# High halves from the scaled tile with the bias at once, low halves two tiles behind the scaling, and the first slot behind each norm waiting tile by tile

## The chip, the core and the metric

The kernel runs on one core of a Trainium2 chip. Its engines work side by side, each through its own list of instructions: TensorE (PE; its weight loads are shown as PEld), VectorE (DVE), ScalarE (ACT), GpSimd (POOL) and SyncE (SP), which only issues DMAs here. They wait for each other by semaphores. The metric is the device time of one execution in microseconds (us), as the median of several runs.

## The reference

One inference step of a two-layer decoder: 256 new tokens of a prompt and 8 tokens of running samples go through the same weights. Layer 0 is a gated DeltaNet and a dense SwiGLU, layer 1 a short gated convolution and an expert SwiGLU (two of eight). Behind each of the four sublayers stands a norm over the 1024 features:

```
def layer_norm(x, g, b):
    mu = mean(x); var = mean((x - mu) ** 2)
    return (x - mu) * rsqrt(var + LN_EPS) * g + b

hp = layer_norm(ALPHA * hp + mixer(hp), ln_g[i, 0], ln_b[i, 0])     # 256 prompt tokens
hp = layer_norm(ALPHA * hp + channel_mixer(hp), ln_g[i, 1], ln_b[i, 1])
# hs, the 8 sample tokens, in the same way
```

Two of these four are touched: the first norm of layer 0, behind which the gate and up projections of the dense SwiGLU follow (x @ w_gu), and the second, behind which the input projection of the short convolution follows (x @ w_in).

## The kernel before, in words

The 264 tokens (256 + 8) stand side by side as columns, the 1024 features as 8 tiles of 128 partitions. `xres[:, k, :]` is feature tile k of the residual stream, 128x264 in float32. To keep float32 accuracy on TensorE each operand is a sum of a high half (rounded by the engine that writes it, type fp32r) and a low half, the rest. A product is three matmuls: weights high by x high, weights high by x low, weights low by x high.

Weights come in slots of 1 MB (128x2048). SP loads slot n into one of 7 buffers `raw`, ScalarE makes `high` in one of 3 buffers (`split_high`, L335), VectorE makes `low` (`split_low`, L340), and TensorE consumes a slot in `dense_slot`. A dense slot has 2 groups (t) of 128 output features. A group first runs over the 8 feature tiles with a pair of matmuls each, L354 (with `xh`, the high half of x) and L355 (with `xl`, the low half), and then over the 8 tiles again with L359 (low weights). When a slot is done, `slot_used` counts up; that frees buffers, so ScalarE and VectorE split the slot 3 further on and SP loads the one 7 further on. `dense_slot` takes an `arrive` function that can wait before each pair of the first group; before the change only the out projection of layer 0 used it.

The norm in this transposed layout: TensorE sums the 8 tiles with a matrix of ones (L1704, mean), VectorE subtracts the mean (L1186), ScalarE squares (L793), TensorE sums again (L1708, variance), ScalarE forms rstd by a logarithm and an exponential (L795, L797), for which it loads a table. Then comes the tail of the norm, which the change is about:

- VectorE scales the 8 tiles by gamma and rstd (L1189), counting `scaled`;
- ScalarE adds the bias in place (L800), counting `x_new`, and one tile behind copies to the high half `xh` (L805, the last at L808), counting `xh_ready`;
- VectorE, once all 8 tiles are scaled, subtracts to get the low half `xl` (L1194), counting `xl_ready`;
- TensorE waits for all high and all low halves (L1712 and L1713 in layer 0, L1747 and L1748 in layer 1) and only then goes on.

Behind the first norm TensorE then transposes the last rows of the DeltaNet's input (L1721, eight small matmuls), which ScalarE copies out (L818, `tail_sb`); the second slot waits for these copies. Then come 11 pairs of gate and up slots. GpSimd waits for all of `x_new` of the first norm (L517) before it loads the state of the samples, which ScalarE reads at L834. The order on every engine is written out by hand: it is the order of the code.

Of the kernel before, what the change touches and what calls it, by code (L numbers as in the profile page):

```python
# [8 lines left out]
KT = D // 128  # L9
# [51 lines left out]
def hybrid_step(nc, x_prompt, x_sample, state_gdn_S, state_gdn_conv, state_sconv, ln_g, ln_b, gdn_w_in,  # L61
# [8 lines left out]
    with ExitStack() as ctx:  # L70
# [546 lines left out]
        def _(act):  # L617
# [168 lines left out]
                act.wait_ge(slot_used, n + 1)  # L786
                split_high(act, n + SPLIT)

            def layer_norm(l, split):
                act.preload_act_table_set("natural_log")  # L790
                for k in range(KT):
                    act.wait_ge(xc_ready, 8 * l + k + 1)
                    act.activation(lnsq[:, k, :], xres[:, k, :], ACT.Square).then_inc(lnsq_ready, 1)  # L793
                act.wait_ge(var_psum, l + 1)
                act.activation(rvar[:, :], bank[5][:, 0:N], ACT.Ln, scale=1.0 / D, bias=eps[:, 1:2]).then_inc(var_inv, 1)  # L795
                act.wait_ge(var_inv, l + 1)
                act.activation(rstd[:, :], rvar[:, :], ACT.Exp, scale=-0.5).then_inc(var_root, 1)  # L797
                for k in range(KT):
                    act.wait_ge(scaled, 8 * l + k + 1)
                    act.activation(xres[:, k, :], xres[:, k, :], ACT.Identity, bias=vecs[:, k, 4 + l:5 + l])\  # L800
                        .then_inc(x_new, 1)
                    if split:
                        if k:
                            act.wait_ge(x_new, 8 * l + k)
                            act.activation(xh[:, k - 1, :], xres[:, k - 1, :], ACT.Copy).then_inc(xh_ready, 1)  # L805
                if split:
                    act.wait_ge(x_new, 8 * l + 8)
                    act.activation(xh[:, KT - 1, :], xres[:, KT - 1, :], ACT.Copy).then_inc(xh_ready, 1)  # L808

            layer_norm(0, True)  # L810

            act.wait_ge(hist_out, 48)
            for i in range(FF // 256):
# [22 lines left out]
            for n in range(DOWN0, SCI0):  # L836
                act.wait_ge(slot_used, n + 1)
                split_high(act, n + SPLIT)
            layer_norm(1, True)

            for i in range(D // 256):
                n = SCI0 + 2 * i
# [75 lines left out]
        def _(dve):  # L918
# [253 lines left out]
                    add_residual(2 * (n - OUT0) + t, 2 * (n % 2) + t)  # L1172
                split_low(dve, n + SPLIT)

            def layer_norm(l, split):
                dve.wait_ge(mean_psum, l + 1)
                if l == 0:
                    dve.wait_ge(zero_out, 16 * (JOBS + 2))
                    dve.wait_ge(gate_out, 48)
                    dve.wait_ge(hist_out, 48)  # L1180
                if l == 1:
                    dve.wait_ge(tail_out, 32)
                step(dve.tensor_scalar(mu[:, :], bank[4][:, 0:N], 1.0 / D, None, ALU.mult))
                step.wait()
                for k in range(KT):
                    dve.tensor_tensor(xres[:, k, :], xres[:, k, :], mu[:, :], ALU.subtract).then_inc(xc_ready, 1)  # L1186
                dve.wait_ge(var_root, l + 1)
                for k in range(KT):
                    dve.scalar_tensor_tensor(xres[:, k, :], xres[:, k, :], vecs[:, k, l:l + 1], rstd[:, :],  # L1189
                                             ALU.mult, ALU.mult).then_inc(scaled, 1)  # L1190
                if split:
                    for k in range(KT):
                        dve.wait_ge(xh_ready, 8 * (l + 2) + k + 1)
                        dve.tensor_tensor(xl[:, k, :], xres[:, k, :], xh[:, k, :].bitcast(F32), ALU.subtract)\  # L1194
                            .then_inc(xl_ready, 1)

            layer_norm(0, True)
            for i in range(FF // 256):
                n = GU0 + 2 * i
                dve.wait_ge(slot_used, n + 1)  # L1200
# [20 lines left out]
            for n in range(DOWN0, SCI0):  # L1221
# [2 lines left out]
                    for d in range(KT):  # L1224
                        add_residual(d, d)
                split_low(dve, n + SPLIT)
            layer_norm(1, True)

            dve.wait_ge(const_ready, 6)
            for i in range(D // 256):  # L1230
# [238 lines left out]
        def _(pe):  # L1469
# [230 lines left out]
            def layer_norm(l):  # L1700
# [7 lines left out]
                    last = pe.matmul(bank[5][:, 0:N], ones[:, :], lnsq[:, k, :], start=k == 0, stop=k == KT - 1)  # L1708
                last.then_inc(var_psum, 1)

            layer_norm(0)
            pe.wait_ge(xh_ready, 24)  # L1712
            pe.wait_ge(xl_ready, 24)  # L1713
            for i in range(FF // 256):
                if i >= 2:
                    pe.wait_ge(gate_silu, 2 * (i - 1))
                    pe.wait_ge(h_ready, 2 * (i - 1))
                if i < 3:
                    for b in range(2):
                        for t in range(4):  # L1720
                            last = pe.transpose(bank[4 * (i % 2) + 2 + b][0:11, 128 * t:128 * t + 128],  # L1721
                                                utail[:, 8 * i + 4 * b + t, :], idn)
                        last.then_inc(tail_psum, 1)
                dense_slot(pe, GU0 + 2 * i, 4 * (i % 2), xh, xl)
                if i < 3:
                    pe.wait_ge(tail_sb, 2 * i + 2)
                dense_slot(pe, GU0 + 2 * i + 1, 4 * (i % 2) + 2, xh, xl)
# [16 lines left out]
                last.then_inc(slot_used, 1)  # L1744
            pe.wait_ge(res_ready, 16)
            layer_norm(1)
            pe.wait_ge(xh_ready, 32)  # L1747
            pe.wait_ge(xl_ready, 32)  # L1748
            for i in range(D // 256):
                if i >= 2:  # L1750
                    pe.wait_ge(c_copied, 2 * (i - 1))
                    pe.wait_ge(u_ready, 2 * (i - 1))
                dense_slot(pe, SCI0 + 2 * i, 4 * (i % 2), xh, xl)
                dense_slot(pe, SCI0 + 2 * i + 1, 4 * (i % 2) + 2, xh, xl)
            for i in range(D // 256):
                pe.wait_ge(c_copied, 6 if i < 2 else 8)
# [168 lines left out]
```

## Time and profile before

| | |
|---|---|
| median of 3 runs | 1688.25 us (1687.16 to 1688.6) |
| the profiled execution | 1687.96 us |
| its span, from the first to the last instruction | 1686.2 us |
| TensorE busy in the span | 1589.6 us, 94% |
| VectorE, ScalarE, GpSimd busy | 1272.0, 1049.7, 96.5 us |
| mean granted clock of TensorE | 0.966 |

All rows below come from the one profiled execution, with times from the start of its span. Busy times overlap, and a busy TensorE isn't one at its peak: what a stage is bound by is read from who waits last in it. The granted clock has two levels, 1.00 (2.4 GHz) and 0.50 (1.2 GHz); a value between them is a stretch in which it changed.

### The profile page before, as it was taken

How to read it: one execution, taken by the hardware profiler on the slowest of the kernel's cores; microseconds unless marked ns; L12 is line 12 of the kernel's file. 1: busy time of each engine (PE TensorE's matmuls, PEld its weight loads, DVE VectorE, ACT ScalarE, POOL GpSimd, SP SyncE). 2: the span in 40 equal slices, each digit the busy share in tenths (PEclk: the TensorE clock that was granted, in tenths of full speed). 3: DMA queues.
4: the chain of work that ended last, by engine and by line, in shares of the span. 5: the costliest groups of instructions: out<-in, count | busy, mean ns of one | idle time of the engine just before them, and what ended most of it. 6: DMA issues, size and time to landing. Idle time of an engine off the chain costs nothing.

```text
span 1686.2 us, 23688 instructions
## 1 busy us (share of the span) xinstructions
PE 1589.6 (94%) x8997; PEld 1379.7 (82%) x8997; DVE 1272.0 (75%) x1234; ACT 1049.7 (62%) x959; POOL 96.5 (6%) x151
## 2 busy tenths in 40 slices
PE   7999997799996999999999999999999999999991
PEld 6889997799996998887887887887887887887881
DVE  5685545377534656888888888888889889889887
ACT  4981424466434333777777777777777777777772
POOL 3105000011000001000000000000000000002001
PEclk9998999899998997999999999999999999999996
DMA  9647603389553552999999999999999999999991
GB/s 269 213 133 229 251 2 113 125 265 320 193 179 123 184 165 82 388 374 340 391 367 347 388 367 350 385 367 350 385 366 351 382 368 353 380 364 359 395 367 64
DMA packets 228273, 480.19 MB, mean 285 GB/s; under 512 B 9660, under 2 KB 69068, under 8 KB 227913
## 3 DMA queue, kind: packets, MB, share of 16 engines
q1 hardware_dynamic: 215904, 438.92, 72.8%
q0 software_dynamic: 11216, 40.06, 7.0%
q10 hardware_dynamic: 1096, 0.41, 0.2%
q8 instruction: 41, 0.67, 0.2%
q14 instruction: 16, 0.13, 0.0%
HBM read 452.82 MB, written 26.77 MB: 284 GB/s over the span
## 4 chain that ended last, share of the span: by engine, by line
PE 88%; ACT 5%; DVE 4%; DMA 1%; issue 1%; DVEq 0%; SPq 0%; ACTq 0%; POOLq 0%
PE bank L1847 12%; PE bank L1848 12%; PE bank L1851 12%; PE bank L1876 11%; PE bank L354 6%; PE bank L355 6%; PE bank L359 6%; PE bank L1882 6%; ACT high L335 2%; PE bank L1606 1%; PE bank L1737 1%; PE bank L1738 1%; PE bank L1743 1%; PE bank L1627 1%; PE bank L1859 1%; DVE low L340 1%
## 5 line engine op out<-in xcount | busy, mean ns | idle before, releaser
L340 DVE TENSOR_TENSOR low<-raw,high 128x2048 fp32r<-128x2048 f32 x408 | 931.2, 2290 | 249.9 <-ACT high L335 249.7
L335 ACT ACTIVATE high<-raw 128x2048 fp32r<-128x2048 f32 x408 | 779.7, 1916 | 284.4 <-PE bank L1851 104.7
L1847 PE MATMUL bank<-high,xgh 128*128 128x512 f32 x896 | 359.7, 401 | 0.0
L1848 PE MATMUL bank<-high,xgl 128*128 128x512 f32 x896 | 355.5, 397 | 0.0
L1851 PE MATMUL bank<-low,xgh 128*128 128x512 f32 x896 | 246.0, 396 | 0.0
L354 PE MATMUL bank<-xh,high 128*128 128x264 f32 x864 | 228.7, 297 | 16.8 <-ACT xh L808 9.3
L355 PE MATMUL bank<-xl,high 128*128 128x264 f32 x864 | 225.6, 294 | 0.0
L1851 PEld LDWEIGHTS bank<-low,xgh 128*128 128x128 f32 x896 | 168.9, 189 | 41.4
L1847 PEld LDWEIGHTS bank<-high,xgh 128*128 128x128 f32 x896 | 169.5, 189 | 38.7
L1848 PEld LDWEIGHTS bank<-high,xgl 128*128 128x128 f32 x896 | 168.8, 188 | 38.8
L354 PEld LDWEIGHTS bank<-xh,high 128*128 128x128 f32 x864 | 171.1, 198 | 19.1 <-ACT xh L808 9.6
L355 PEld LDWEIGHTS bank<-xl,high 128*128 128x128 f32 x864 | 171.3, 198 | 1.0 <-issue 1.0
L1876 PE MATMUL bank<-high,hth 128*128 128x512 f32 x448 | 141.4, 397 | 8.1 <-DVE htl L1414 8.1
L1876 PE MATMUL bank<-high,htl 128*128 128x512 f32 x448 | 140.5, 395 | 0.0
L359 PE MATMUL bank<-xh,low 128*128 128x264 f32 x864 | 124.5, 287 | 1.3 <-DVE low L340 1.3
L1882 PE MATMUL bank<-low,hth 128*128 128x512 f32 x448 | 122.3, 394 | 0.0
L359 PEld LDWEIGHTS bank<-xh,low 128*128 128x128 f32 x864 | 114.6, 192 | 1.6 <-DVE low L340 1.6
L1876 PEld LDWEIGHTS bank<-high,hth 128*128 128x128 f32 x448 | 83.5, 188 | 28.8 <-issue 10.0
L1882 PEld LDWEIGHTS bank<-low,hth 128*128 128x128 f32 x448 | 84.4, 188 | 20.2
L1876 PEld LDWEIGHTS bank<-high,htl 128*128 128x128 f32 x448 | 84.5, 189 | 19.8
L899 ACT ACTIVATE sgx<-bank 128x512 f32<-128x512 f32 x56 | 33.5, 599 | 42.6 <-PE bank L1851 42.5
L597 POOL TENSOR_TENSOR flag<-flag 128x1 f32<-128x1 f32 x1 | 2.2, 2218 | 880.5 <-DMA tok<-ysb 880.5
(370 smaller groups left out, 1473.5 us busy)
## 6 DMA issues: line engine op xcount, KB each, us to landing
raw<-in_moe_w_gu_dram SPq DMA_DIRECT2D x224, 1024.0 KB, 5.3
raw<-in_moe_w_down_dram SPq DMA_DIRECT2D x115, 1024.0 KB, 5.4
raw<-in_ffn_w_gu_dram SPq DMA_DIRECT2D x22, 1024.0 KB, 7.0
raw<-in_gdn_w_in_dram SPq DMA_DIRECT2D x16, 1024.0 KB, 8.5
tok<-zeros POOLq DMA_DIRECT2D x26, 512.0 KB, 17.4
raw<-in_sc_w_in_dram SPq DMA_DIRECT2D x12, 1024.0 KB, 5.1
raw<-in_ffn_w_down_dram SPq DMA_DIRECT2D x11, 1024.0 KB, 5.0
tok<-ysb SPq DMA_DIRECT2D x9, 512.0 KB, 6.0
```

The source lines that it names most:

```text
L335: eng.activation(high[:, n % SPLIT, :], raw[:, n % RAW, :], ACT.Copy).then_inc(high_ready, 1)
L340: eng.tensor_tensor(low[:, n % RAW, :], raw[:, n % RAW, :], high[:, n % SPLIT, :].bitcast(F32), ALU.subtract).then_inc(low_ready, 1)
L354: pe.matmul(out, wh[:, k, f], act_h[:, k, :], start=k == 0, stop=False)
L355: pe.matmul(out, wh[:, k, f], act_l[:, k, :], start=False, stop=False)
L359: last = pe.matmul(out, wl[:, k, f], act_h[:, k, :], start=False, stop=k == KT - 1)
L899: act.activation(sgx[:, u % 2, :], bank[2 * (u % 2)][:, :], ACT.Silu).then_inc(sgx_ready, 1)
L1606: last = pe.matmul(heads(4 * c + g)[:, h % 4, :], AT[:, c, h, :], T[:, c, h, :], start=True, stop=True)
L1847: pe.matmul(out, xgh[:, 4 * kh + k, :], wh[:, k, :], start=kh + k == 0, stop=False)
L1848: pe.matmul(out, xgl[:, 4 * kh + k, :], wh[:, k, :], start=False, stop=False)
L1851: last = pe.matmul(out, xgh[:, 4 * kh + k, :], wl[:, k, :], start=False, stop=kh == 1 and k == 3)
L1876: pe.matmul(bank[4 + g][:, :], src[:, u % 2, hs], wh[:, k, 512 * g:512 * g + 512], start=u + kh + k == 0 and src is hth, stop=False)
L1882: last = pe.matmul(bank[4 + g][:, :], hth[:, u % 2, hs], wl[:, k, 512 * g:512 * g + 512], start=False, stop=u == UNITS - 1 and kh + k == 2)
```

## The change

In the tail of the norm ScalarE makes the high half of tile k straight from the scaled tile, with the bias added in the same pass. VectorE makes the low half of tile k - 2 right behind the scaling of tile k, as (scaled tile + bias) - high half. ScalarE adds the bias to `xres` in place only after all eight high halves, tile k once low half k has been made. TensorE doesn't wait for the whole norm any more: the first group of the first slot waits before each pair for that tile's halves, and the transposes behind the first norm wait for nothing of it.

```diff
@@ ScalarE, layer_norm(l)
                 for k in range(KT):
                     act.wait_ge(scaled, 8 * l + k + 1)
+                    act.activation(xh[:, k, :], xres[:, k, :], ACT.Identity, bias=vecs[:, k, 4 + l:5 + l]).then_inc(xh_ready, 1)
+                for k in range(KT):
+                    act.wait_ge(xl_ready, 8 * (l + 2) + k + 1)
                     act.activation(xres[:, k, :], xres[:, k, :], ACT.Identity, bias=vecs[:, k, 4 + l:5 + l])\
                         .then_inc(x_new, 1)
-                    if split:
-                        if k:
-                            act.wait_ge(x_new, 8 * l + k)
-                            act.activation(xh[:, k - 1, :], xres[:, k - 1, :], ACT.Copy).then_inc(xh_ready, 1)
-                if split:
-                    act.wait_ge(x_new, 8 * l + 8)
-                    act.activation(xh[:, KT - 1, :], xres[:, KT - 1, :], ACT.Copy).then_inc(xh_ready, 1)
@@ VectorE, layer_norm(l)
                 dve.wait_ge(var_root, l + 1)
+                def low_half(k):
+                    dve.wait_ge(xh_ready, 8 * (l + 2) + k + 1)
+                    dve.scalar_tensor_tensor(xl[:, k, :], xres[:, k, :], vecs[:, k, 4 + l:5 + l], xh[:, k, :].bitcast(F32),
+                                             ALU.add, ALU.subtract).then_inc(xl_ready, 1)
+
                 for k in range(KT):
                     dve.scalar_tensor_tensor(xres[:, k, :], xres[:, k, :], vecs[:, k, l:l + 1], rstd[:, :],
                                              ALU.mult, ALU.mult).then_inc(scaled, 1)
-                if split:
-                    for k in range(KT):
-                        dve.wait_ge(xh_ready, 8 * (l + 2) + k + 1)
-                        dve.tensor_tensor(xl[:, k, :], xres[:, k, :], xh[:, k, :].bitcast(F32), ALU.subtract)\
-                            .then_inc(xl_ready, 1)
+                    if k >= 2:
+                        low_half(k - 2)
+                low_half(KT - 2)
+                low_half(KT - 1)
@@ TensorE
+            def norm_arrives(l):
+                def arrive(k):
+                    pe.wait_ge(xh_ready, 8 * (l + 2) + k + 1)
+                    pe.wait_ge(xl_ready, 8 * (l + 2) + k + 1)
+                return arrive
+
             layer_norm(0)
-            pe.wait_ge(xh_ready, 24)
-            pe.wait_ge(xl_ready, 24)
...
-                dense_slot(pe, GU0 + 2 * i, 4 * (i % 2), xh, xl)
+                dense_slot(pe, GU0 + 2 * i, 4 * (i % 2), xh, xl, norm_arrives(0) if i == 0 else None)
...
             layer_norm(1)
-            pe.wait_ge(xh_ready, 32)
-            pe.wait_ge(xl_ready, 32)
...
-                dense_slot(pe, SCI0 + 2 * i, 4 * (i % 2), xh, xl)
+                dense_slot(pe, SCI0 + 2 * i, 4 * (i % 2), xh, xl, norm_arrives(1) if i == 0 else None)
```

On VectorE the tail of the first norm stands like this before (var_root says that rstd is there):

```order
L1189 SCALAR_TENSOR_TENSOR xres<-xres,vecs,rstd 128x264 [waits var_root]
L1189 SCALAR_TENSOR_TENSOR xres<-xres,vecs,rstd 128x264 x7
L1194 TENSOR_TENSOR xl<-xres,xh 128x264 [waits xh_ready] x8
```

and like this after, where the scaling is L1190 and the low half L1186:

```order
L1190 SCALAR_TENSOR_TENSOR xres<-xres,vecs,rstd 128x264 [waits var_root]
L1190 SCALAR_TENSOR_TENSOR xres<-xres,vecs,rstd 128x264 x2
L1186 SCALAR_TENSOR_TENSOR xl<-xres,vecs,xh 128x264 [waits xh_ready]
L1190 SCALAR_TENSOR_TENSOR xres<-xres,vecs,rstd 128x264
L1186 SCALAR_TENSOR_TENSOR xl<-xres,vecs,xh 128x264 [waits xh_ready]
...
L1190 SCALAR_TENSOR_TENSOR xres<-xres,vecs,rstd 128x264
L1186 SCALAR_TENSOR_TENSOR xl<-xres,vecs,xh 128x264 [waits xh_ready] x3
```

Each low half from the first on now stands between two scalings, and a wait for ScalarE stands ahead of each scaling from the fourth on. On TensorE, from the variance sums of the first norm on, before:

```order
L1708 MATMUL bank<-lnsq,ones 128x264 [waits lnsq_ready] x8
L1721 MATMUL bank<-ident,utail 11x128 [waits xl_ready,xh_ready]
L1721 MATMUL bank<-ident,utail 11x128 x7
L354 MATMUL bank<-xh,high 128x264 [waits high_ready]
L355 MATMUL bank<-xl,high 128x264
L354 MATMUL bank<-xh,high 128x264
L355 MATMUL bank<-xl,high 128x264
```

and after (the transposes are L1725):

```order
L1708 MATMUL bank<-lnsq,ones 128x264 [waits lnsq_ready] x8
L1725 MATMUL bank<-ident,utail 11x128 x8
L354 MATMUL bank<-xh,high 128x264 [waits xl_ready,xh_ready,high_ready]
L355 MATMUL bank<-xl,high 128x264
L354 MATMUL bank<-xh,high 128x264 [waits xl_ready,xh_ready]
L355 MATMUL bank<-xl,high 128x264
```

The wait for the halves has moved from the transposes to the pairs, and every pair of the first group has its own. On ScalarE, after, from rstd on:

```order
L797 ACTIVATE rstd<-rvar 128x264 [waits var_inv]
L800 ACTIVATE xh<-xres,vecs 128x264 [waits scaled] x8
L803 ACTIVATE xres<-xres,vecs 128x264 [waits xl_ready] x8
L814 ACTIVATE tail_nat<-bank 11x512 [waits tail_psum,hist_out]
L814 ACTIVATE tail_nat<-bank 11x512 [waits tail_psum]
L820 ACT_TABLE_LOAD
L820 ACTIVATE sg<-bank 128x264 [waits slot_used]
```

Before, the two passes of a tile alternated; now the eight passes in place stand behind the eight high halves, with the tail copies behind them as before.

## Rows read from the trace of the kernel before

**Rows 1.** The page's span, and groups by line: busy, mean ns, idle before.

```profile
span 1686.2 us, 23688 instructions
L359 PE MATMUL bank<-xh,low 128*128 128x264 f32 x864 | 124.5, 287 | 1.3 <-DVE low L340 1.3
L1189 DVE SCALAR_TENSOR_TENSOR xres<-xres,vecs,rstd 128x264 f32<-128x264 f32 x16 | 6.6, 487 | 10.1 <-ACT rstd L797 10.1
```

**Rows 2.** Waits, 285 to 320 us: total, times, longest.

```profile
PE bank L1721 <- DVE xl L1194: 9.3, 1, 9.3
```

**Rows 3.** Timeline of VectorE, first norm: start, duration, instruction, count, idle before.

```profile
302.01 3.32 DVE L1189 SCALAR_TENSOR_TENSOR xres<-xres,vecs,rstd 128x264 f32<-128x264 f32 x8 [5.91 <-ACT rstd L797]
305.25 1.86 DVE L1194 TENSOR_TENSOR xl<-xres,xh 128x264 fp32r<-128x264 f32 x5
...
308.11 0.78 DVE L1194 TENSOR_TENSOR xl<-xres,xh 128x264 fp32r<-128x264 f32 x2 [0.28 <-ACT xh L805]
```

**Rows 4.** Timeline of ScalarE, first norm and the start of the gate slots.

```profile
302.54 0.92 ACT L800 ACTIVATE xres<-xres,vecs 128x264 f32<-128x264 f32 x2 [0.56 <-DVE xres L1189]
...
303.68 0.50 ACT L800 ACTIVATE xres<-xres,vecs 128x264 f32<-128x264 f32 x1
304.08 0.41 ACT L805 ACTIVATE xh<-xres 128x264 fp32r<-128x264 f32 x1
...
307.98 0.41 ACT L808 ACTIVATE xh<-xres 128x264 fp32r<-128x264 f32 x1
...
311.54 1.28 ACT L824 ACT_TABLE_LOAD   x1
...
327.40 1.05 ACT L818 ACTIVATE tail_nat<-bank 11x512 f32<-11x512 f32 x2
...
339.99 2.44 ACT L834 ACTIVATE dB<-dB,kS 128x128 f32<-128x128 f32 x8
```

**Rows 5.** Timeline of TensorE, first norm.

```profile
294.20 5.52 PE L1708 MATMUL bank<-lnsq,ones 128*128 128x264 f32 x16 [2.11 <-ACT lnsq L793]
309.03 1.87 PE L1721 MATMUL bank<-ident,utail 128*11 128x128 f32 x8 [9.31 <-DVE xl L1194]
310.55 0.57 PE L354 MATMUL bank<-xh,high 128*128 128x264 f32 x1
...
314.21 1.42 PE L359 MATMUL bank<-xh,low 128*128 128x264 f32 x8
315.47 0.28 PE L354 MATMUL bank<-xh,high 128*128 128x264 f32 x1
315.59 0.28 PE L355 MATMUL bank<-xl,high 128*128 128x264 f32 x1
```

**Rows 6.** Timeline of VectorE, second norm.

```profile
525.67 3.32 DVE L1189 SCALAR_TENSOR_TENSOR xres<-xres,vecs,rstd 128x264 f32<-128x264 f32 x8 [4.22 <-ACT rstd L797]
...
531.77 0.78 DVE L1194 TENSOR_TENSOR xl<-xres,xh 128x264 fp32r<-128x264 f32 x2 [0.28 <-ACT xh L805]
```

**Rows 7.** Timeline of TensorE, second norm.

```profile
532.64 0.56 PE L354 MATMUL bank<-xh,high 128*128 128x264 f32 x1 [9.26 <-ACT xh L808]
533.00 0.42 PE L355 MATMUL bank<-xl,high 128*128 128x264 f32 x1
533.22 0.42 PE L354 MATMUL bank<-xh,high 128*128 128x264 f32 x1
...
536.30 1.34 PE L359 MATMUL bank<-xh,low 128*128 128x264 f32 x8
```

**Rows 8.** Windows of 1 us, first norm: busy (x count) by engine, clock, DMA, GB/s.

```profile
297.00:298.00 1.00, 1.00 (x5) 0.76 (x3) 0.00 (x0) 0.00 (x0) 0.00 (x0) 0.62 0.00 0
...
304.00:305.00 1.00, 0.00 (x0) 0.00 (x0) 1.00 (x4) 1.00 (x4) 0.00 (x0) 0.80 0.00 0
...
314.00:315.00 1.00, 1.00 (x7) 1.00 (x7) 0.00 (x0) 0.00 (x0) 0.00 (x0) 0.58 1.06 315
```

**Rows 9.** The same, second norm (PE, PEld, DVE, ACT, POOL in that order).

```profile
536.00:537.00 1.00, 1.00 (x8) 1.00 (x7) 0.00 (x0) 0.00 (x0) 0.00 (x0) 0.65 0.82 307
```

**Rows 10.** Timeline of GpSimd, first norm.

```profile
308.46 0.89 POOL L520 DMA_DIRECT2D s0f<-in_state_gdn_S_dram  x1 [50.02 <-ACT xres L800]
```

More of the change, by code:

```diff
@@ L787, in _, with layer_norm @@
                 split_high(act, n + SPLIT)
-            def layer_norm(l, split):
+            def layer_norm(l):
                 act.preload_act_table_set("natural_log")
@@ L799, in layer_norm @@
                     act.wait_ge(scaled, 8 * l + k + 1)
+                    act.activation(xh[:, k, :], xres[:, k, :], ACT.Identity, bias=vecs[:, k, 4 + l:5 + l]).then_inc(xh_ready, 1)
+                for k in range(KT):
+                    act.wait_ge(xl_ready, 8 * (l + 2) + k + 1)
                     act.activation(xres[:, k, :], xres[:, k, :], ACT.Identity, bias=vecs[:, k, 4 + l:5 + l])\
                         .then_inc(x_new, 1)
-                    if split:
-                        if k:
-                            act.wait_ge(x_new, 8 * l + k)
-                            act.activation(xh[:, k - 1, :], xres[:, k - 1, :], ACT.Copy).then_inc(xh_ready, 1)
-                if split:
-                    act.wait_ge(x_new, 8 * l + 8)
-                    act.activation(xh[:, KT - 1, :], xres[:, KT - 1, :], ACT.Copy).then_inc(xh_ready, 1)
-            layer_norm(0, True)
+            layer_norm(0)
             act.wait_ge(hist_out, 48)
@@ L838, in _ @@
                 split_high(act, n + SPLIT)
-            layer_norm(1, True)
+            layer_norm(1)
             for i in range(D // 256):
@@ L1173, in _, with layer_norm @@
                 split_low(dve, n + SPLIT)
-            def layer_norm(l, split):
+            def layer_norm(l):
                 dve.wait_ge(mean_psum, l + 1)
@@ L1190, in layer_norm @@
                                              ALU.mult, ALU.mult).then_inc(scaled, 1)
-                if split:
-                    for k in range(KT):
-                        dve.wait_ge(xh_ready, 8 * (l + 2) + k + 1)
-                        dve.tensor_tensor(xl[:, k, :], xres[:, k, :], xh[:, k, :].bitcast(F32), ALU.subtract)\
-                            .then_inc(xl_ready, 1)
-            layer_norm(0, True)
+                    if k >= 2:
+                        low_half(k - 2)
+                low_half(KT - 2)
+                low_half(KT - 1)
+            layer_norm(0)
             for i in range(FF // 256):
@@ L1226, in _ @@
                 split_low(dve, n + SPLIT)
-            layer_norm(1, True)
+            layer_norm(1)
             dve.wait_ge(const_ready, 6)
```

## The prediction, as it was made before the changed kernel ran

> **What bounds the kernel now.** I read the waits of the stretch around the first norm first, then the timelines of VectorE, ScalarE and TensorE in it, then the same for the second norm, and last the stretches of 1 us for the granted clock. In a dense slot TensorE hardly waits: its 864 matmuls with low halves (L359) were held 1.3 us in all by a split [rows 1]. Behind the first norm it stands still for 9.3 us, and what ends this is the last low half of x [rows 2]. So the tail of each norm lies on the path that sets the end, and a microsecond gained there on TensorE should stay gained, since the slots behind it are bound by TensorE.
>
> The tail runs like this in the first norm. VectorE scales eight tiles from 302.01 and only then makes low halves from 305.25; the last two end at 308.11 + 0.78 = 308.89 [rows 3]. It is not VectorE alone: ScalarE does two passes a tile, bias in place and then the high half [rows 4], and its last high half is what the last low halves wait for. TensorE starts at 309.03 with eight transposes of the tail rows, reaches the slot's first pair at 310.55 after 1.52 us, and its first low-weight matmul (L359) at 314.21 [rows 5]. The second norm has no transposes: scaling from 525.67, last low half at 531.77 + 0.78 = 532.55 [rows 6], first pair at 532.64, L359 at 536.30 [rows 7].
>
> **The change, part by part.** I work out when L359 of the first group starts, since from there on the instructions are the same as before.
>
> VectorE: eight scalings of mean 487 ns [rows 1] take 3.32 us in a row, so one starts (3.32 - 0.487) / 7 = 0.405 us behind the other [rows 3]. The new low half has the same kind of operands (two tensors and a column of scalars) and isn't in the trace. Bounds: the old low half starts (1.86 - 0.43) / 4 = 0.358 us apart [rows 3], and without any overlap it would be 0.487. I take 0.405, that of the scaling, the same form of instruction. The row is now S0 S1 S2 L0 S3 L1 ... S7 L5 L6 L7, 16 instructions. L7 starts 15 x 0.405 = 6.08 behind the first and ends 0.49 later: 302.01 + 6.56 = 308.57 in the first norm, 525.67 + 6.56 = 532.23 in the second. That is only 0.32 us earlier than before in each: VectorE becomes the limit of the tail, and the larger gain must come from TensorE. With 0.487 for all, L7 ends at 302.01 + 16 x 0.487 = 309.80, 1.23 us later in each norm, 2.5 in all. With 0.358 for the low halves, ScalarE's relay (next) leaves at most 0.15 us in each, 0.3 in all.
>
> ScalarE: high half k is now one pass with the bias, 0.50 us long, a next one 0.40 behind it [rows 4]; the scaled tiles come 0.81 apart, so it keeps up. Does the relay stall VectorE? S0 ends at 302.50, high half 0 runs 302.54 to 303.04, and L0 is due at 302.01 + 3 x 0.405 = 303.23. S7 starts at 302.01 + 12 x 0.405 = 306.87 and ends at 307.36, its high half ends at about 307.90, L7 is due at 308.09. There is 0.15 to 0.19 us to spare, so two tiles of distance are just enough, and I put the stall at nothing. A full relay at each tile would take 0.49 + 0.04 + 0.50 + 0.04 + 0.49 = 1.56 us, one of the rivals.
>
> TensorE: pair k starts when its low half is there. At the low clock a pair takes 2 x 0.22 = 0.44 us [rows 7], against 0.81 between arrivals, so only the last pairs queue: L5, L6, L7 come 0.405 apart. From the end of the last low half to L359 I take what the lone first pair of the second norm shows: 532.64 - 532.55 = 0.09, then 0.36 to its second matmul, then 0.22 to the next, 0.67 us [rows 6, 7]. L359 starts at 308.57 + 0.67 = 309.24 instead of 314.21, 4.97 earlier, and at 532.23 + 0.67 = 532.90 instead of 536.30, 3.40 earlier. Sum 8.37 us. Of the 4.97, 1.52 are the transposes: they no longer stand behind the wait for xl and run in the idle time after the variance sums.
>
> The clock takes part of that back. It falls at about 304.6 [rows 8] in the idle time, when the new pairs have barely begun; so pairs and L359 start at the low level (1.2 GHz). Before, it rose again at 314.84 (0.58 in that microsecond means 0.84 us low) and at 536.70 [rows 8, 9]: L359 had just begun, only 0.63 and 0.40 us behind its start were low. A matmul takes 0.220 us low and 0.122 high [rows 5], so a low microsecond loses 0.445: 0.28 and 0.18 us. The rises that I can read came 3.6 us (294.20 to 297.76), 4.1 us (532.64 to 536.70) and 5.8 us (309.03 to 314.84) behind the first matmul after an idle time [rows 5, 7, 8, 9]. Now TensorE works without a pause from pair 5 on, 307.85 and 531.51 (L5's end and 0.09). I take the middle one, 4.1: rises at 311.9 and 535.6, 2.7 us behind L359, a loss of 1.2 us in each norm against 0.28 and 0.18 before: 1.0 and 1.0 given back. Bounds: with 3.6, 0.8 in each; with 5.8, 1.7 and 1.8; and if the spaced pairs already bring the rise, nothing is lost and the 0.46 of before is won besides.
>
> [...]
>
> What is moved behind. ScalarE writes x in place after all high halves, pass k waiting for L k: from 307.81, 0.405 apart, the last from about 310.64 to 311.15; before, it had finished at 308.39. Behind it are queued the two tail copies, 1.05 together [rows 4], to 312.2, and a table load of 1.28 to 313.5. TensorE's second slot waits for these copies; its first slot ends at 309.24 + 8 x 0.22, then some four matmuls low and twenty high, about 314.3, or 313.15 with the clock high throughout. So 1 to 2 us cover the later copies, and I cost them at nothing; the SiLU behind the table load is not asked for by TensorE until two pairs of slots later. GpSimd's state loads wait for the last x: they leave 2.7 us later than at 308.46 [rows 10], and ScalarE first reads them at 339.99 [rows 4], some 25 us behind. SP's queue waits on slots alone and moves with TensorE.
>
> Sum: 8.37 - 2.0 = 6.4 us. The profiled execution took 1687.96 us (span 1686.2, and 1.76 around it), which gives 1681.6; it lies 0.29 below the median of the runs, so by the median it would be 1681.9.
>
> **The rivals.** Late clock: the rise is as late as the slowest row in both norms, 5.8 us. Then 4.4 us behind L359 are low, 1.97 lost in each, 3.5 more than before, 4.9 us gained: 1683.1. For it: the first norm did this, with the transposes ahead. Against: two of three rises came sooner.
> Early clock: the spaced pairs, some 0.44 us of work in 0.81, bring the rise before L359: 8.8 gained, 1679.1. Nothing in the trace shows a stretch like that at the low level, for or against.
> Serial relay: VectorE stands still for ScalarE at every tile, 1.56 instead of 0.81 us a step. Five such steps lie ahead of L5, 5 x 0.75 = 3.75 in each norm, 7.5 in all against the 6.4: 1.1 slower, 1689.1, no change that can be measured. For it: the margin is only 0.15 us. Against: a wait that is already satisfied shows no cost, the old low halves with one each started 0.358 apart [rows 3].
> Slower: the same relay with slower handovers. Above 0.81 + 6.4 / 10 = 1.45 us a step the kernel loses, above 0.81 + (6.4 + 3.4) / 10 = 1.79 by more than 0.2%. At 1.9 us it is 10 x 1.09 = 10.9 against 6.4, 4.5 slower: 1692.5. Three instructions of 0.49, 0.50 and 0.49 leave 0.42 for two handovers, 0.21 each, where the rows show 0.04 (302.50 to 302.54).
>
> **How the numbers follow.** Forecast 0.60, late clock 0.17, early clock 0.12, serial relay 0.08, slower 0.03. The time is 1681.6. The range goes from the early clock, 1679.0, to 1684.5, which takes in the late clock with 1.4 us of the bound on VectorE's pace; beyond it lie the relays and the worst of that pace. The measurement tells about 0.2%, 3.4 us, from no change. Faster than that: forecast, early and nearly all of the late clock, 0.88; within it: serial relay and the rest, 0.09; slower 0.03.
>
> **What would show it.** In the profile after: low halves and scalings alternate on VectorE 0.40 apart, with no idle over 0.1 us, the last ending 6.5 to 6.6 us behind the first scaling; pairs on TensorE 0.8 apart; the transposes right behind the variance sums; L359 at 7.2 us behind the first scaling; the granted clock back at 2.4 GHz about 2.7 us behind L359's start; no wait for the tail copies. I am wrong if VectorE shows gaps in front of low halves, if the clock rises outside 0 to 4.4 us behind L359, or if TensorE in the first slots stands for ScalarE.

## The result, and the profile after

| | median | runs | profiled execution | its span | mean granted clock |
|---|---|---|---|---|---|
| before | 1690.01 us | 6 (1687.16 to 1691.93) | 1687.96 | 1686.2 | 0.966 |
| changed | 1678.46 us | 6 (1674.81 to 1680.17) | 1677.33 | 1675.6 | 0.970 |

The ratio is 0.9931, with a 95% interval of 0.9915 to 0.9946: 11.7 us less by the ratio, 11.55 by the medians, where 6.4 were forecast. The time of 1678.46 lies below the range, which began at 1679.0. The median of before is over six runs now, three of them beside the changed kernel.

The tail of the norm does what was worked out. VectorE in the first norm, timeline of the changed kernel (start, duration, instruction, count, idle before), against [rows 3]:

```profile
304.63 1.30 DVE L1190 SCALAR_TENSOR_TENSOR xres<-xres,vecs,rstd 128x264 f32<-128x264 f32 x3 [5.91 <-ACT rstd L797]
305.85 0.48 DVE L1186 SCALAR_TENSOR_TENSOR xl<-xres,vecs,xh 128x264 fp32r<-128x264 f32 x1
306.26 0.49 DVE L1190 SCALAR_TENSOR_TENSOR xres<-xres,vecs,rstd 128x264 f32<-128x264 f32 x1
...
309.49 0.48 DVE L1190 SCALAR_TENSOR_TENSOR xres<-xres,vecs,rstd 128x264 f32<-128x264 f32 x1
309.90 1.30 DVE L1186 SCALAR_TENSOR_TENSOR xl<-xres,vecs,xh 128x264 fp32r<-128x264 f32 x3
```

Scalings and low halves start 0.40 us apart and no row has an idle time; the last ends at 309.90 + 1.30 = 311.20, 6.57 us behind the first scaling (6.56 forecast). ScalarE, against [rows 4]:

```profile
305.16 1.33 ACT L800 ACTIVATE xh<-xres,vecs 128x264 fp32r<-128x264 f32 x3 [0.56 <-DVE xres L1190]
306.78 0.52 ACT L800 ACTIVATE xh<-xres,vecs 128x264 fp32r<-128x264 f32 x1 [0.29 <-DVE xres L1190]
...
310.43 3.34 ACT L803 ACTIVATE xres<-xres,vecs 128x264 f32<-128x264 f32 x8
313.68 1.05 ACT L814 ACTIVATE tail_nat<-bank 11x512 f32<-11x512 f32 x2
```

From the fourth on it waits 0.29 us for each scaled tile, so it has room. TensorE, against [rows 5]:

```profile
302.18 1.04 PE L1725 MATMUL bank<-ident,utail 128*11 128x128 f32 x8
306.48 0.36 PE L354 MATMUL bank<-xh,high 128*128 128x264 f32 x1 [3.26 <-ACT xh L800]
306.68 0.28 PE L355 MATMUL bank<-xl,high 128*128 128x264 f32 x1
307.29 0.56 PE L354 MATMUL bank<-xh,high 128*128 128x264 f32 x1 [0.33 <-ACT xh L800]
...
311.98 1.96 PE L359 MATMUL bank<-xh,low 128*128 128x264 f32 x8
313.74 0.42 PE L354 MATMUL bank<-xh,high 128*128 128x264 f32 x1
...
315.85 1.13 PE L359 MATMUL bank<-xh,low 128*128 128x264 f32 x8
```

The last row is L359 of the second group, which in the kernel before stands here:

```profile
317.42 1.15 PE L359 MATMUL bank<-xh,low 128*128 128x264 f32 x8
```

The transposes stand behind the variance sums, pairs come 0.81 apart, and L359 starts 311.98 - 304.63 = 7.35 us behind the first scaling, where it was 314.21 - 302.01 = 12.20 [rows 3, 5] and 7.23 was forecast (from the end of the last low half to L359 it is 0.78 us, not 0.67). In the second norm (timelines of VectorE and TensorE) it is 7.35 again, against 10.63 [rows 6, 7]:

```profile
525.32 1.30 DVE L1190 SCALAR_TENSOR_TENSOR xres<-xres,vecs,rstd 128x264 f32<-128x264 f32 x3 [4.22 <-ACT rstd L797]
...
532.67 1.96 PE L359 MATMUL bank<-xh,low 128*128 128x264 f32 x8
```

So L359 came 4.85 and 3.28 us earlier (4.97 and 3.40 forecast). The granted clock, in windows of 1 us (busy by engine, clock, DMA share, GB/s), against [rows 8, 9]:

```profile
314.00:315.00 1.00, 1.00 (x10) 1.00 (x10) 0.00 (x0) 0.98 (x3) 0.53 (x1) 0.97 0.00 0
...
535.00:536.00 1.00, 1.00 (x7) 1.00 (x6) 0.00 (x0) 0.00 (x0) 0.24 (x1) 0.54 0.97 225
```

It is back at 2.4 GHz at 314.06 and 535.92, 2.1 and 3.3 us behind L359 (2.7 forecast in both). In these terms nothing is off by more than 0.6 us. The rest of the 11.7 us is somewhere else, and comparing stage by stage shows where: most of it at the gather of the expert rows, 340 us behind the first norm, which the change doesn't touch. There TensorE picks the token rows for the experts by 48 small matmuls with a one-hot matrix; behind them come 20 transposes and then the first expert matmul. TensorE's timeline there, before and then changed:

```profile
650.56 13.32 PE L1825 MATMUL bank<-onehot,xn 128*128 128x128 f32 x48 [0.81 <-DVE onehot L1350]
...
667.99 0.78 PE L1847 MATMUL bank<-high,xgh 128*128 128x512 f32 x1
```

```profile
646.66 8.48 PE L1827 MATMUL bank<-onehot,xn 128*128 128x128 f32 x48 [0.80 <-DVE onehot L1350]
...
658.18 0.49 PE L1849 MATMUL bank<-high,xgh 128*128 128x512 f32 x1 [0.71 <-DVE xgl L1398]
```

The same 48 matmuls take 13.3 or 8.5 us. Windows of before and of the changed kernel say why (the granted clock is the third number from the end):

```profile
645.00:646.00 1.00, 1.00 (x7) 1.00 (x6) 1.00 (x1) 0.00 (x0) 0.00 (x0) 0.54 0.00 0
...
652.00:653.00 1.00, 1.00 (x7) 0.76 (x6) 0.90 (x7) 0.00 (x0) 1.00 (x1) 0.88 0.00 0
...
669.00:670.00 1.00, 1.00 (x4) 0.81 (x3) 1.00 (x1) 0.00 (x0) 0.00 (x0) 0.59 0.00 0
```

```profile
641.00:642.00 1.00, 1.00 (x8) 1.00 (x7) 0.97 (x3) 0.10 (x1) 0.00 (x0) 0.63 0.00 0
...
648.00:649.00 1.00, 1.00 (x8) 0.76 (x7) 0.86 (x7) 0.00 (x0) 0.91 (x1) 1.00 0.00 0
```

Before, the clock rose at 645.92, fell again at 652.76, 2.2 us into the gather, and stayed at 1.2 GHz for 17 us, though TensorE was never idle in them. In the changed kernel it rose at 641.74 and stayed up. From the gather's start to the first expert matmul it is 17.43 us before and 11.52 after, and 0.71 of the 11.52 is now a wait for VectorE's low half of the gathered rows: with the clock high TensorE is no longer the one that comes last there. Another low stretch, at the first slot of the convolution's output projection (from 608.38 before), has gone too, and one at the start of the down projection (from 443.76 after) is new:

```profile
608.00:609.00 1.00, 1.00 (x8) 1.00 (x8) 0.88 (x1) 1.00 (x3) 0.00 (x0) 0.69 1.04 406
```

```profile
443.00:444.00 1.00, 0.45 (x3) 0.45 (x3) 0.50 (x2) 1.00 (x2) 0.00 (x0) 0.88 0.40 115
...
606.00:607.00 1.00, 1.00 (x9) 1.00 (x10) 1.00 (x1) 0.64 (x2) 0.07 (x1) 1.00 1.04 406
```

### The profile page after: what moved, and what is told of

Same layout as the page of the kernel before. It is cut to its first block, busy times and chain, and to the rows that moved or that the text cites. A ratio compares the mean times of both kernels' runs of the same rounds, so it can differ in the third digit from the quotient of the medians.

```text
span 1675.6 us, 23702 instructions
## 1 busy us (share of the span) xinstructions
PE 1589.7 (95%) x8997; PEld 1378.2 (82%) x8997; DVE 1272.3 (76%) x1234; ACT 1052.4 (63%) x959; POOL 96.3 (6%) x151
## 4 chain that ended last, share of the span: by engine, by line
PE 88%; DVE 5%; ACT 4%; DMA 1%; issue 1%; DVEq 0%; SPq 0%; ACTq 0%; POOLq 0%
PE bank L1849 13%; PE bank L1853 13%; PE bank L1850 13%; PE bank L1878 11%; PE bank L354 6%; PE bank L359 6%; PE bank L355 6%; PE bank L1884 6%; ACT high L335 2%; PE bank L1741 1%; DVE low L340 1%; PE bank L1742 1%; PE bank L1606 1%; PE bank L1747 1%; PE bank L1627 1%; PE bank L1861 1%
## 5 line engine op out<-in xcount | busy, mean ns | idle before, releaser
L359 PE MATMUL bank<-xh,low 128*128 128x264 f32 x864 | 126.2, 290 | 1.4 <-DVE low L340 1.4
L359 PEld LDWEIGHTS bank<-xh,low 128*128 128x128 f32 x864 | 116.2, 194 | 1.6 <-DVE low L340 1.6
L1878 PEld LDWEIGHTS bank<-high,hth 128*128 128x128 f32 x448 | 83.5, 188 | 28.8 <-issue 10.0
```

Source lines behind the costliest of these rows:

```text
L359: last = pe.matmul(out, wl[:, k, f], act_h[:, k, :], start=False, stop=k == KT - 1)
L1878: pe.matmul(bank[4 + g][:, :], src[:, u % 2, hs], wh[:, k, 512 * g:512 * g + 512], start=u + kh + k == 0 and src is hth, stop=False)
```

## The experiments

Theory 1: the norms save what the rows gave, some 6 us, and the rest is the clock at the gather. 1a, added later: whether it falls there depends on the moment at which TensorE gets there behind the last rise of the clock. Its rivals: theory 2, the norms alone save the whole 11 us, by the new order of the halves; 1b, only the idle gap ahead of the gather counts. The `keep_running(n, b)` of the edits issues n filler transposes of an identity matrix into bank b, whose result no one reads; the kernel before has some already.

**TensorE's part alone** (shown for the first norm; the second has the same edit).

```diff
 # kernel before
-            pe.wait_ge(xh_ready, 24)
-            pe.wait_ge(xl_ready, 24)
-                dense_slot(pe, GU0 + 2 * i, 4 * (i % 2), xh, xl)
+                dense_slot(pe, GU0 + 2 * i, 4 * (i % 2), xh, xl, norm_arrives(0) if i == 0 else None)
```

> TensorE's part alone: the kernel before, but the first slot behind each norm waits tile by tile and the transposes wait for nothing of the norm; ScalarE and VectorE as before. The low halves then come as before, the last at 6.88 us behind the first scaling, with the last three 0.36 and 0.7 apart. L359 at 6.88 + 0.67 = 7.6 us behind the first scaling, against 12.2 (first norm) and 10.6 (second) before and 7.35 in the changed kernel. Theory 1 (the saving at the norms is what was predicted, some 6 us, and the rest comes from the clock at the gather of the expert rows, which falls or not with the moment that stage is reached): 5 to 6 us less than before from the norms, and another 6 where the gather's clock holds; its profile tells which, gather (L1825) 13.3 us low or 8.5 us high. Theory 2 (the norms alone save the whole 11 us, by the new order of the halves): clearly less gain here than in the changed kernel, even where the gather takes the same time.

Measured: 1678.77 us, ratio 0.9936 (0.9919 to 0.9952), the gain of the whole change within the intervals. L359 7.70 and 7.48 us behind the first scaling, 4.50 and 3.15 earlier than before where the whole change has 4.85 and 3.28; gather 8.48 us. So TensorE's part, the wait tile by tile with the transposes ahead of it, is nearly all of it.

**The halves alone** (again in both norms).

```diff
 # changed kernel
             layer_norm(0)
+            pe.wait_ge(xh_ready, 24)
+            pe.wait_ge(xl_ready, 24)
-                dense_slot(pe, GU0 + 2 * i, 4 * (i % 2), xh, xl, norm_arrives(0) if i == 0 else None)
+                dense_slot(pe, GU0 + 2 * i, 4 * (i % 2), xh, xl)
```

> The halves alone: ScalarE and VectorE as in the changed kernel, TensorE waits for the whole norm as before. The last low half ends 6.6 instead of 6.9 us behind the first scaling, so L359 0.2 to 0.3 us earlier in each norm. Theory 1: 0.4 to 0.6 us of gain at the norms, which no run can tell, and all further difference is the gather's, 0 or 5 to 7 us, with the matmuls of the gather in the profile at 8.5 or 13.3 us. Theory 2: several us of gain with the gather as before.

Measured: 1689.05 us, ratio 0.9994 (0.9984 to 1.0004). Its gather, in TensorE's timeline, is the slow one:

```profile
647.59 13.39 PE L1825 MATMUL bank<-onehot,xn 128*128 128x128 f32 x48 [0.81 <-DVE onehot L1350]
```

The order of the halves by itself gives 0.1 us by the medians; the interval allows up to 2.7. In its first norm the first pair comes 8.22 us behind the first scaling instead of 8.54, the 0.3 expected. L359 comes 1.2 earlier there, and the rest of that is the clock, which rose at 311.80, 1.1 us ahead of L359. That the halves save the 11 us falls with these two; that the norms do, with the next two.

**Feeding TensorE ahead of the gather**, in the kernel before and in the changed one.

```diff
             pe.wait_ge(xn_ready, 6)
-            keep_running(12, 6)
+            keep_running(20, 6)
```

> The kernel before with 20 instead of 12 filler transposes ahead of the gather, which fill the 0.8 us in which TensorE waits for onehot there. Theory 1: the clock doesn't fall at the gather, which takes 8.5 instead of 13.3 us, and the first expert slot starts some 6 us earlier: 5 to 7 us less than before, 0.1 to 0.3 of it lost to the filler. Theory 2: the clock at the gather costs nothing that counts, or falls all the same: within 1 us of before.

> The changed kernel with the same 20 fillers. Theory 1: its gather was mostly at the high clock already, so within 1.5 us of the changed kernel's 1678.5, and 6 us (5 to 7.5) below the kernel before with the fillers: that is the change's own saving. Theory 2: 10 to 12 us below the kernel before with the fillers.

Measured: before, fed, 1684.70 us, ratio 0.9971 (0.9961 to 0.9981); changed, fed, 1678.23, ratio 0.9934 (0.9922 to 0.9947). The gather of before, fed:

```profile
654.05 8.48 PE L1825 MATMUL bank<-onehot,xn 128*128 128x128 f32 x48
```

Filling 0.8 us of idle time gives the kernel before 4.5 us, a little less than the 5 to 7 expected, and the changed one nothing that can be told. The difference of the two fed kernels, 6.5 us, is what the change is worth with the gather at one clock, to some 2.5 us either way by the two intervals; the forecast was 6.4. The low stretches elsewhere are not the same in the two, see below.

**Only the transposes moved ahead of the wait.**

```diff
 # kernel before
             layer_norm(0)
-            pe.wait_ge(xh_ready, 24)
-            pe.wait_ge(xl_ready, 24)
...
+                if i == 0:
+                    pe.wait_ge(xh_ready, 24)
+                    pe.wait_ge(xl_ready, 24)
                 dense_slot(pe, GU0 + 2 * i, 4 * (i % 2), xh, xl)
```

> The kernel before with one edit: behind the first norm the eight transposes stand ahead of the wait for the halves. Theory 1 (the norms save what the sum of rows says): 1.5 us leave the path there, L359 at 10.7 instead of 12.2 us behind the first scaling, less what more low clock behind it costs, so 0.5 to 1.5 us of gain, with the gather as before at 13.3 us. Theory 2 (an arrival at the gather that is earlier by any amount frees its clock): 6 us or more.

Measured: 1682.87 us, ratio 0.9959 (0.9944 to 0.9975), about 7 us for an edit that takes 1.9 us off L359 (10.31 us behind the first scaling). I expected 1.5 at most: the miss has the same cause as that of the prediction, the gather took 8.48 us. By its time alone this run meets the rival in that expectation, that any earlier arrival at the gather frees its clock; the next two runs speak against it, in which a later arrival freed the clock and an earlier one lost it.

**Moving the moment of the gather**, by four transposes more in the kernel before and three fewer in the changed one.

```diff
 # kernel before
-            keep_running(24, 3)
+            keep_running(28, 3)
 # changed kernel
-            keep_running(24, 3)
+            keep_running(21, 3)
```

> The kernel before with 28 instead of 24 filler transposes behind the router's matmuls, which is 0.5 us more work on TensorE, and nothing else. Theory 1a (the clock falls at the gather by the moment at which TensorE reaches it after the last rise, 4.63 and 4.69 us where it fell, 4.92 to 5.6 where it held): 5.1 us now, the clock holds, the gather takes 8.5 us, and the kernel is 4 to 6 us faster with more work. Theory 1b (the moment doesn't matter, the idle gap of 0.8 us does): the gap is as it was, the gather 13.3 us, 0 to 0.6 slower.

> The changed kernel with 21 instead of 24 fillers there, some 0.5 us less work. Theory 1a: the gather begins 4.3 to 4.5 us behind the rise, the clock falls in it, 13.3 us, and the kernel is 4 to 6 us slower with less work. Theory 1b: the gather as in the changed kernel, 8.5 us, 0 to 0.5 us faster.

Measured: before with more work 1685.35 us, ratio 0.9967 (0.9955 to 0.9980), faster; changed with less work 1681.78, ratio 0.9951 (0.9936 to 0.9966), by the medians 3.3 us slower than the changed kernel's 1678.46. Its interval overlaps with that of the changed kernel (0.9915 to 0.9946), so by time alone this second one isn't clear of the noise; its profile is. Of each, the microsecond with the last rise and the gather (windows, timeline), first before with 28:

```profile
650.00:651.00 1.00, 1.00 (x10) 1.00 (x9) 1.00 (x1) 0.00 (x0) 0.00 (x0) 0.81 0.00 0
```

```profile
655.46 8.48 PE L1825 MATMUL bank<-onehot,xn 128*128 128x128 f32 x48 [0.81 <-DVE onehot L1350]
```

and changed with 21:

```profile
642.00:643.00 1.00, 1.00 (x8) 1.00 (x7) 0.96 (x3) 0.10 (x1) 0.00 (x0) 0.62 0.00 0
```

```profile
647.33 13.26 PE L1827 MATMUL bank<-onehot,xn 128*128 128x128 f32 x48 [0.81 <-DVE onehot L1350]
```

The gap of 0.81 us is there in both; what differs is the time from the rise to the gather, 5.08 and 4.57 us. 1a holds against 1b, each time against the sign of the work. From the router to the gather the edits made 0.43 us more and 0.33 us less. The second was less than the 4 to 6 us expected; its six runs spread from 1680.33 to 1685.43 and their mean granted clocks from 0.963 to 0.969, where the profiled one had 0.964 and the changed kernel's six 0.969 to 0.972. So the gather was probably not slow in all, which one profile can't settle.

**Second profiles of both kernels, unchanged.**

> The kernel before, unchanged, for a second profile. Theory 1a: the gather starts less than 4.8 us behind the last rise of the clock again and takes 13.3 us; the stretch before the first norm differs by up to 5 us from the first profile. If the gather takes 8.5 us here, its clock is luck in the kernel before, too, and its median hides two cases.

> The changed kernel, unchanged, for a second profile. Theory 1a: the gather starts more than 4.8 us behind the last rise and takes 8.5 us; L359 7.35 us behind the first scaling in both norms; the time between 1674.8 and 1680.2.

Measured: 1693.15 and 1680.99 us in one run each. TensorE's timeline, before and then changed:

```profile
655.77 13.30 PE L1825 MATMUL bank<-onehot,xn 128*128 128x128 f32 x48 [0.81 <-DVE onehot L1350]
```

```profile
650.12 8.48 PE L1827 MATMUL bank<-onehot,xn 128*128 128x128 f32 x48 [0.81 <-DVE onehot L1350]
```

The gather repeats in both. The changed kernel's time lies 0.8 above the 1674.8 to 1680.2 expected. No run of before that was made beside the experiments was under 1686.09. All profiles together, with times in us (S is the first scaling of a norm; the rise is the last one of the clock ahead of the gather, from windows of 1 us):

```
kernel             start-S1  S1-L359  S1-S2   S2-L359  S2-router  rise-gather  clock falls in it  gather-expert
before              302.0    12.20   223.66   10.63    110.89      4.64        yes                17.43
before again        307.1    12.21   223.70   10.64    110.97      4.61        yes                17.41
halves alone        301.9    11.00   223.63   10.31    109.41      4.69        yes                17.50
changed, 21         305.2     7.35   221.05    7.35    107.43      4.57        yes                16.66
before, 28          306.4    12.21   223.69   10.64    110.93      5.08        no                 12.31
transposes only     305.2    10.31   221.19   10.61    110.68      4.90        no                 12.28
TensorE's part      307.6     7.70   221.16    7.48    106.06      5.60        no                 11.52
changed             304.6     7.35   220.69    7.35    107.35      4.92        no                 11.52
changed again       307.7     7.35   220.98    7.36    107.41      4.86        no                 11.67
before, fed         305.2    11.18   223.80   10.64    111.02      4.39        no (no gap)        11.53
changed, fed        301.4     7.35   220.78    7.35    107.34      4.85        no (no gap)        11.53
```

With the gap of 0.8 us in place the clock fell in all four profiles with up to 4.69 us and in none of the five from 4.86 on; with the gap filled it held at 4.39 too. It takes both, the gap and the moment. No run shows where between 4.69 and 4.86 it turns, nor why there.

**Feeding the norms.** A version that might beat both: filler transposes (into bank 6, which no one uses there) where TensorE idles in the two norms: 14 between the sums, 24 behind the transposes of the first, 34 behind the variance sums of the second.

```diff
 # changed kernel, with the 20 fillers ahead of the gather
                 last.then_inc(mean_psum, 1)
+                if l < 2:
+                    keep_running(14, 6)
...
+                if i == 0:
+                    keep_running(24, 6)
...
             layer_norm(1)
+            keep_running(34, 6)
```

> The changed kernel with filler transposes on TensorE where it waits in the two norms (14 between the two sums, 24 and 34 behind the variance sums) and 20 instead of 12 ahead of the gather. If the low clock at the norms is the idle time's doing, it stays high there: L359 still 7.2 us behind the first scaling, since VectorE sets that, but its second group 1.0 us behind the first norm's row (8.3 us instead of 11.2 behind the first scaling), 3 us of gain in each norm less 0.5 where fillers delay the sums: 4 to 6 us below the changed kernel. If fillers don't hold the clock: within 1 us of the changed kernel, or above it.

Measured: 1677.13 us, ratio 0.9921 (0.9906 to 0.9936): 1.3 below the changed kernel, not the 4 to 6 expected. TensorE's timeline, then the windows that show the clock's fall:

```profile
295.86 3.83 PE L1710 MATMUL bank<-lnsq,ones 128*128 128x264 f32 x16 [0.59 <-ACT lnsq L793]
...
300.40 2.78 PE L1477 MATMUL bank<-ident 128*128 128x128 f32 x24
303.83 0.36 PE L354 MATMUL bank<-xh,high 128*128 128x264 f32 x1 [0.65 <-ACT xh L800]
...
525.45 0.36 PE L354 MATMUL bank<-xh,high 128*128 128x264 f32 x1 [0.43 <-ACT xh L800]
```

```profile
306.00:307.00 1.00, 0.75 (x2) 0.50 (x2) 1.00 (x4) 0.71 (x2) 0.00 (x0) 0.63 0.00 0
...
528.00:529.00 1.00, 0.76 (x3) 0.49 (x4) 1.00 (x4) 0.54 (x2) 0.00 (x0) 0.56 0.00 0
```

The fillers hold the clock up to the first pair, and then it falls at 306.26, in the midst of the spaced pairs, with 0.33 us of idle time between them; in the second norm it falls at 528.13, again among the pairs. Two effects nearly cancel in the time: the variance sums of the first norm run at the high clock (3.83 us instead of the 5.52 of [rows 5]), so the first scaling comes 1.7 us sooner behind the start of the mean sums, but the low weights of the second group come 0.75 and 0.35 us later than in the changed kernel. By time alone the two kernels can't be told apart. The Trainium skill (TensorE: Matmul & The Clock Gate, section Loop structure matters more than you think) warns of a long wait between every two matmuls, which lets the engine's clock drop. The trace agrees with that and shows it for waits that aren't long, 0.33 us for a pair. So the gaps between pairs were filled as well, with four transposes in one kernel and three in another; both also have 28 instead of 24 fillers behind the transposes of the first norm, and the second norm has its 34 as before:

```diff
                 def arrive(k):
+                    if 1 <= k <= 5:
+                        keep_running(4, 6)
                     pe.wait_ge(xh_ready, 8 * (l + 2) + k + 1)
```

> As the changed kernel with fillers in the norms and ahead of the gather, and now also four filler transposes between the pairs of the first group (0.46 us of work in gaps of about 0.57), 28 instead of 24 behind the first variance sums. In the kernel with fillers but bare pairs the clock fell in the midst of the spaced pairs. Theory 1b (spaced pairs themselves bring the clock down): it now stays high from the variance sums on, the second group of the slot starts 8.3 us behind the first scaling instead of 11.4 and 11.8 (a pair's weight load and matmuls at the high clock, L359 7.1 to 7.4), 3 us in each norm: 5 to 6 us below the changed kernel, 1672 to 1674. If pairs don't matter: as with bare pairs, 1677. Where the clock is low all the same, each filler takes 0.19 us and delays the pairs: up to 2 us slower.

> The same with three fillers between pairs, 0.35 us of work in the gap. Theory 1b: the clock holds in most executions, 0 to 2 us above the kernel with four; with a fallen clock no pair is delayed, so the spread is smaller.

Measured: 1672.48 us, ratio 0.9898 (0.9882 to 0.9914), with four; 1672.86, ratio 0.9896 (0.9877 to 0.9915), with three. TensorE's timeline with four, and a window:

```profile
301.41 0.36 PE L354 MATMUL bank<-xh,high 128*128 128x264 f32 x1 [0.21 <-ACT xh L800]
301.62 0.29 PE L355 MATMUL bank<-xl,high 128*128 128x264 f32 x1
301.74 0.60 PE L1477 MATMUL bank<-ident 128*128 128x128 f32 x4
302.22 0.36 PE L354 MATMUL bank<-xh,high 128*128 128x264 f32 x1
...
306.59 1.14 PE L359 MATMUL bank<-xh,low 128*128 128x264 f32 x8
307.56 0.28 PE L354 MATMUL bank<-xh,high 128*128 128x264 f32 x1
...
519.58 0.36 PE L354 MATMUL bank<-xh,high 128*128 128x264 f32 x1 [0.43 <-ACT xh L800]
```

```profile
306.00:307.00 1.00, 1.00 (x8) 0.89 (x9) 0.12 (x1) 1.00 (x4) 0.00 (x0) 1.00 0.08 16
...
522.00:523.00 1.00, 1.00 (x9) 0.90 (x8) 1.00 (x4) 0.53 (x2) 0.00 (x0) 1.00 0.00 0
```

The clock stays high here through the tails of both norms. In the second norm only the fillers between the pairs differ from the kernel with bare pairs (34 ahead and 0.43 us of idle time in both), so there it is the spaced pairs that brought the clock down; with three fillers between pairs it stays high in both tails too. In the first norm L359 starts 7.03 us behind the first scaling (299.56) and the second group at 8.00. The expectation compared unlike things: its 11.4 and 11.8 are where the second group's low weights start in the changed kernel, and the group itself starts at 9.11. Like for like the low weights of the second group come at 9.95 instead of 11.22 and at 9.94 instead of 11.71: 3.0 us in both norms, not 6. The 5 to 6 us expected were met all the same, 6.0: another 1.7 is the first norm's variance sums at the high clock, and low stretches elsewhere went or moved (none in the profile with four near 443.76, one at 438.10 in that with three). Three fillers do as well as four, 0.4 us apart by the medians; that they make the spread smaller, as expected, doesn't show (1667.07 to 1676.05, and 1666.77 to 1676.5 with four).

## Why the prediction was wrong

At the two norms the mechanism was right and the sizes close; what failed is the step in its first paragraph, that a microsecond gained at the norm "should stay gained, since the slots behind it are bound by TensorE", and with it the sentence that from L359 on the instructions are the same as before. They are the same, but the clock under them isn't: the sum put every stage behind the norms at nothing, and the gather alone gave 5.9 us up to the first expert matmul and 0.8 in the experts.

- L359 earlier by 8.37: measured 4.85 + 3.28 = 8.13. The pace of 0.405 for the new low halves, no stall of VectorE, no wait for the tail copies: as forecast.
- The clock's share at the norms, 2.0: the second group's low weights came at 15.41 and 13.75 us behind the first scaling before and at 11.22 and 11.71 after, 4.19 and 2.04 earlier, together 6.23. So 8.13 - 6.23 = 1.9: 0.7 and 1.2 given back where 1.0 and 1.0 were forecast. That the sum comes out so near is partly luck.
- Sum 6.4: the two fed kernels differ by 6.5. This agreement, too, is partly luck. In their profiles the norms give 2.8 and 2.1 us by the second group's low weights (14.10 to 11.28 and 13.90 to 11.76), 5.0 in all, since the clock rose 9.9 instead of 12.8 us behind the first scaling in the first norm of the fed kernel before; some 1.5 us is a low stretch at 612.12 that only this one has. The norms are worth 5.0 or 6.2 us in the two pairs of profiles, by where the clock stands.
- The profiles of before and of the changed kernel differ as follows, stage by stage: start to the first scaling +2.6; from there to the second norm -3.0, that is -4.2 and 1.2 lost to the low stretch at 443.76; to the router -3.5, of it 2.0 the norm's and the rest the low stretch at 608.38 that went; the gather to the first expert matmul -5.9; the experts -0.8. Together -10.6, as the spans.
- The +2.6 ahead of everything is chance: this stretch took 301.4 to 307.7 us in the eleven profiles of the table, in no order with the change. In the two profiles of before it makes 5.1 of their 5.2 us, in those of the changed kernel 3.1 of 3.7; the three runs that I had lay within 1.4.
- The rivals moved the clock only right behind L359. The case that came, a gain that changes the clock in a stage far behind, wasn't among them, and no row of it was read. The rows for it were in the trace: the gather's clock fell 2.2 us into it and its matmuls took 13.3 us, 4.8 more than in the changed kernel.
- The relays and the slower case: nothing of them showed. VectorE had no idle row.
- Two small slips, on which nothing hangs: with a rise after 3.6 us the first norm gives back 0.7, not 0.8, and ScalarE's read at 339.99 lies 28.8 us behind the end of its passes, not some 25.

What stays open: why TensorE's position against the rise of the clock is so steady in one kernel (4.61 and 4.64 before, 4.86 and 4.92 changed) though the time to reach the first norm varies by 6 us. I suppose that each low stretch ties the work to the moment of its end, since the work done in it is what varies; no run tested this.

## What to carry to other kernels

Where TensorE changes between two clocks, a shift of a few tenths of a microsecond can be worth several in a stage that wasn't touched. Before pricing an edit look for the stages in which the clock is low and those that stand just at an idle gap, and give the range room for their flip, in both directions; to measure the edit itself, fill the gaps in both kernels and compare those. Work that is spread tile by tile over a wait starts early but brings the clock down unless the gaps are filled, here with transposes that no one reads. Fillers don't make two kernels equal in all their low stretches, so compare stage by stage too.

## What the runs showed of the hardware that I had not expected

- Once low, the clock stayed at 1.2 GHz for 17 us (before, 652.76 to 669.82), through the rest of the gather's 48 small matmuls, 20 transposes and the first expert matmuls, with TensorE's row busy all along, while with the clock high the same 48 took 8.5 instead of 13.3 us and kept it there.
- 0.43 us more on TensorE ahead of the gather made a kernel 5.5 us faster. 0.33 less made another 3.3 us slower by the medians, which isn't clear of the noise, but its profile shows the slow gather.
- Transposes hold the clock at 2.4 GHz: with 14 and 28 of them and four between pairs it did not fall in the first norm, and in that profile the low stretch at the start of the down projection was gone as well. With three between pairs it was not, from 438.10 on.
